# Late attention: how the softmax reciprocals reach the output's rows, by diagonals from GpSimd or by a transpose and one product

## The reference

```python
# kind A: dense, 6 query heads on 2 key heads, normalised and rotated
# kind B: window of 128 tokens to either side, with a sink
m = jnp.maximum(jnp.max(s, axis=-1, keepdims=True), sk)
p = jnp.exp(s - m)
denom = jnp.sum(p, axis=-1, keepdims=True) + jnp.exp(sk - m)
p = p / denom
# kind C: dense, 4 heads, keys from a low-rank projection
p = softmax(s)
# all kinds: o = p v, times silu(gate); then x + concat(oa, ob, oc) @ w_out
```

## Time and profile before

| | us |
|---|---|
| median of three runs | 1826.12 |
| lowest and highest | 1824.75, 1828.1 |
| the profiled execution | 1826.74 |
| its span | 1825.0 |
| PE busy, of the span | 1765.7 |
| DVE busy | 801.9 |
| ACT busy | 723.6 |
| POOL busy | 604.0 |
| mean granted clock of PE | 0.988 |

### The profile page before, as it was taken

How to read it: one execution, slowest core, us unless ns; L and a number is a source line. 1 busy time by engine, 2 the same in 40 slices (tenths; PEclk the granted TensorE clock), 3 DMA queues, 4 the chain that set the end, 5 groups by cost and what they waited for, 6 DMA issues and landing times.

```text
span 1825.0 us, 25256 instructions
## 1 busy us (share of the span) xinstructions
PE 1765.7 (97%) x10862; PEld 1390.1 (76%) x10862; DVE 801.9 (44%) x1342; ACT 723.6 (40%) x1228; POOL 604.0 (33%) x182
## 2 busy tenths in 40 slices
PE   8999999999999999998999999989999999999997
PEld 5778899988888888877888888877684478776456
DVE  8756646623123121114670143145446654526653
ACT  5656665433233332233331222234426533345541
POOL 3534210333333434432454444424332114333112
PEclk9999999999999999998999999989999999999998
DMA  5121200326223323222222232213220012211001
GB/s 205 70 93 24 72 3 25 132 70 191 79 95 104 123 70 110 96 93 69 93 92 93 97 111 93 92 70 140 70 83 10 1 48 97 93 69 47 1 1 47
DMA packets 37504, 144.71 MB, mean 79 GB/s; under 512 B 3155, under 2 KB 15835, under 8 KB 23696
## 3 DMA queue, kind: packets, MB, share of 16 engines
q1 hardware_dynamic: 18944, 121.53, 18.8%
q10 hardware_dynamic: 18448, 21.57, 3.9%
HBM read 140.93 MB, written 5.30 MB: 80 GB/s over the span
## 4 chain that ended last, share of the span: by engine, by line
PE 87%; DVE 5%; ACT 4%; issue 1%; DMA 1%; ACTq 0%; POOL 0%; SPq 0%; POOLq 0%; DVEq 0%
PE bank L407 56%; PE bank L1145 6%; PE bank L613 5%; PE bank L418 4%; PE bank L2196 3%; PE bank L2220 3%; PE bank L2203 2%; DVE WK L978 1%; PE bank L1653 1%; PE bank L1629 1%; PE bank L2149 1%; ACT WK L2330 1%; ACT w_part L365 1%; PE bank L2228 1%; DMA WK<-wgate 1%
## 5 line engine op out<-in xcount | busy, mean ns | idle before, releaser
L407 PE MATMUL bank<-x_part,w_part 128*128 128x512 f32 x3216 | 746.8, 392 | 1.5 <-ACT WK L2309 0.8
L407 PEld LDWEIGHTS bank<-x_part,w_part 128*128 128x128 f32 x3216 | 601.0, 188 | 135.4 <-issue 10.7
L2660 POOL TENSOR_TENSOR w_part<-RAW,w_part 128x2048 fp32r<-128x2048 f32 (+1 forms) x90 | 404.2, 4493 | 678.4 <-ACT w_part L365 678.4
L365 ACT ACTIVATE w_part<-RAW 128x2048 fp32r<-128x2048 f32 (+1 forms) x90 | 165.8, 1842 | 175.5 <-PE bank L407 138.0
L2660 POOL TENSOR_TENSOR w_part<-WK,w_part 128x2048 fp32r<-128x2048 f32 (+1 forms) x30 | 123.7, 4124 | 246.9 <-ACT w_part L365 246.9
L407 PE MATMUL bank<-f_part,w_part 128*128 128x512 f32 x768 | 174.4, 389 | 0.0
L407 PEld LDWEIGHTS bank<-f_part,w_part 128*128 128x128 f32 x768 | 144.1, 188 | 29.9
L1145 PE MATMUL bank<-WK 64*64 64x64 f32 (+1 forms) x1456 | 103.4, 249 | 4.8 <-ACT WK L1311 2.5
L1145 PEld LDWEIGHTS bank<-WK 64*64 64x64 f32 (+1 forms) x1456 | 99.0, 163 | 7.3 <-ACT WK L1311 2.6
L978 DVE SCALAR_TENSOR_TENSOR WK<-bank,COL,WK 128x510 f32<-128x510 f32 (+1 forms) x96 | 71.7, 749 | 48.6 <-ACT WK L920 45.9
L2677 POOL TENSOR_TENSOR WK<-BASE,WK 128x1024 f32<-128x1024 f32 x16 | 30.4, 1898 | 167.5 <-DVE WK L2503 167.5
(11 more groups left out here) (286 smaller groups left out, 2236.1 us busy)
## 6 DMA issues: line engine op xcount, KB each, us to landing
RAW<-wts SPq DMA_DIRECT2D x83, 1024.0 KB, 4.8
WK<-wts SPq DMA_DIRECT2D x23, 1024.0 KB, 4.8
WK<-scratch ACTq DMA_DIRECT2D x16, 256.0 KB, 2.7
WK<-decay_rows ACTq DMA_DIRECT2D x14, 256.0 KB, 6.6
RAW<-wts SPq DMA_DIRECT2D x7, 512.0 KB, 3.5
WK<-wts SPq DMA_DIRECT2D x7, 512.0 KB, 3.4
scratch<-bias_rows ACTq DMA_DIRECT2D x4, 768.0 KB, 8.8
WK<-xT SPq DMA_DIRECT2D x4, 512.0 KB, 7.3
```

What stands on the lines that cost most here:

```text
L365: act.eng.activation(high_part(i), raw_part(i), ACT.Copy).then_inc(*act.did(("hi", i)))
L407: mm = pe.eng.matmul(b[:, :], W[w][:, k, c:c + P], src[x][k], start=start and k == 0 and n == 0, stop=stop and k == kn - 1 and n == 2)
L2660: eng.tensor_tensor(low_part(i), raw_part(i), high_part(i).bitcast(F32), ALU.subtract).then_inc(w_split, 1)
```

## The change

The reciprocals of a pair (128 queries by 8 columns: two heads by four tiles) are no longer spread by diagonals. VectorE splits them into a rounded copy and a remainder, side by side in a 128x16 tile (`INV2`). PE turns that to sixteen rows of 128 (`turn_inverses`, behind the first `av`, round 4m+6). VectorE lays the rows out to 16 rows of 512, each row zero outside its own tile (`inverse_rows`, round 4m+6). One fp32r product with a 16x128 matrix of zeros and ones (`HEAD_OF`) adds the two parts and puts them on the head's 64 rows (`spread`, now in round 4m+8, in front of the last `av`). `gated` moves on to round 4m+9, in front of `out`. The masks are made once per layer in round 1 (`row_masks`). The diagonals and their waits leave POOL's list.

```diff
+            def turn_inverses(m):
+                b = job((L, "rt", m), SPREAD_BANK)
+                pe.wait_ge(*at((L, "ri", m)))
+                E.transpose(b[0:16, 0:P], INV2[m % 2][:, :].bitcast(F32), ident).then_inc(*pe.did(("pe", (L, "rt", m))))
+
             def spread(m):
                 b = job((L, "sp", m), SPREAD_BANK)
-                pe.wait_ge(*at((L, "ridiag", m)))
-                for o in range(2):
-                    mm = E.matmul(b[64 * o:64 * o + 64, :], ones[:, 0:64], SPREAD[:, TT * o:TT * o + TT, :], start=True, stop=True)
-                mm.then_inc(*pe.did(("pe", (L, "sp", m))))
+                pe.wait_ge(*at((L, "rows", m)))
+                E.matmul(b[:, :], HEAD_OF[:, :, :].rearrange("p o c -> p (o c)"), INVR[:, :, :].rearrange("p t c -> p (t c)"), start=True, stop=True)\
+                    .then_inc(*pe.did(("pe", (L, "sp", m))))
...
                 if 0 <= m and u < 3:
                     kind = heads[2 * m][5]
+                    if u == 2:
+                        spread(m)
                     av(m, ((0, 3), (1,), (2,))[u] if kind == "B" else ((0, 1), (2,), (3,))[u])
-                    if u == 1:
-                        spread(m)
+                    if u == 0:
+                        turn_inverses(m)
...
-                    if m >= 2:
-                        dve.wait_ge(*at(("pe", (L, "sp", m - 2))))
...
-                    V.reciprocal(ri, sm).then_inc(*dve.did(*([(L, "ri", m)] if n % 2 else [])))
+                    V.reciprocal(ri, sm).then_inc(*dve.did())
+                both, parts2 = LST[:, 80 + 8 * (m % 2):88 + 8 * (m % 2)], INV2[m % 2]
+                dve.wait_ge(*dve.last())
+                if m >= 2:
+                    dve.wait_ge(*at(("pe", (L, "rt", m - 2))))
+                V.tensor_copy(parts2[:, 0:8], both).then_inc(*dve.did())
+                dve.wait_ge(*dve.last())
+                V.tensor_tensor(parts2[:, 8:16], both, parts2[:, 0:8].bitcast(F32), ALU.subtract).then_inc(*dve.did((L, "ri", m)))
+
+            def row_masks():
+                dve.wait_ge(*at(("pe", (L, "uk", 3))))
+                e16 = ident[0:16, 0:16]
+                V.tensor_reduce(TILE_OF[0:16], e16.rearrange("p (g t) -> p t g", t=TT), AX, ALU.add).then_inc(*dve.did())
+                V.tensor_reduce(QUARTER[0:16], e16.rearrange("p (g t) -> p g t", t=TT), AX, ALU.add).then_inc(*dve.did())
+                dve.wait_ge(*dve.last())
+                first, second = (QUARTER[0:16, 2 * i:2 * i + 2].unsqueeze(2).broadcast_to([16, 2, 64]) for i in range(2))
+                V.tensor_tensor(HEAD_OF[:, :, :], first, second, ALU.add).then_inc(*dve.did())
+
+            def inverse_rows(m):
+                dve.wait_ge(*at(("pe", (L, "rt", m))))
+                V.tensor_tensor(INVR[:, :, :], ps((L, "rt", m))[0:16, 0:P].unsqueeze(1).broadcast_to([16, TT, P]),
+                                TILE_OF[0:16].unsqueeze(2).broadcast_to([16, TT, P]), ALU.mult).then_inc(*dve.did((L, "rows", m), free=(L, "rt", m)))
...
+                    row_masks()
...
-                if i >= 8 and (i - 8) % TT == 0 and (i - 8) // TT < len(heads) // 2:
-                    gated((i - 8) // TT)
+                if i >= 6 and (i - 6) % TT == 0 and (i - 6) // TT < len(heads) // 2:
+                    inverse_rows((i - 6) // TT)
                 if i >= 9 and (i - 9) % TT == 0 and (i - 9) // TT < len(heads) // 2:
+                    gated((i - 9) // TT)
                     out((i - 9) // TT)
...
-            def inverse_diagonal(L, m):
...
-                if subs[i][:2] in last_ahead:
-                    inverse_diagonal(last_ahead[subs[i][:2]], 0)
                 low(i)
-                if subs[i][:2] in last_ahead:
-                    for m in range(1, len(heads) // 2):
-                        inverse_diagonal(last_ahead[subs[i][:2]], m)
```

More of the change, by code:

```diff
@@ L2095, in build @@
         GATE_BANKS = (0, 1, 2, 3), (4, 5, 6, 7)
-        SPREAD = wk(35584, 2 * TT, P)
+        INV2 = [nc.alloc_sbuf_tensor_at(name=f"inverse_sums{i}", shape=[P, 16], dtype=F32R, offset=wk_base + 4 * (37376 + 16 * i)) for i in range(2)]
+        INVR = nc.alloc_sbuf_tensor_at(name="inverse_rows", shape=[16, TT, P], dtype=F32R, offset=wk_base + 4 * 35584)
+        HEAD_OF = nc.alloc_sbuf_tensor_at(name="head_of_row", shape=[16, 2, 64], dtype=F32R, offset=wk_base + 4 * 36096)
+        TILE_OF = wk(36224, 4)
+        QUARTER = wk(36228, 4)
         LGP = wk(12288, 6, S)
```

## The result

The changed kernel takes 1829.39 us in the median of 20 runs (1827.34 to 1833.48); the kernel before, in 20 runs beside them, 1824.18. The ratio is 1.0027, with a 95% interval of 1.0020 to 1.0034: slower by 4.9 us, give or take 1.3. The forecast was no change, 1826.1, with a range up to 1829.3. It stood on the median of three runs of the kernel before, 1826.12, which is 1.9 above the median of 20; counted from one base the forecast missed by the whole 4.9 us.

What follows compares the result with a forecast made beforehand. TensorE held 87% of the chain, but VectorE's lateness set the pace in rounds 1 mod 4. Gains and costs by pair, with masks, summed to -0.02 us a layer, -0.04 in both, on 1826.12: 1826.1 us, range 1822.3 to 1829.3.

Steps and rivals of the forecast that it cites:

- the price of TensorE's two steps: Per pair, product 0.23 us and transpose 0.11 replace the spread's 0.86: 0.52 saved where TensorE sets the pace.
- my sum: All pairs' gains and costs plus masks: -0.02 us a layer, -0.04 in both, giving 1826.1 us.
- three signs of being wrong: Attention's 111.4 us changes by over 1.8; 4m+7 maximum late outside pairs 1, 4, 6; transposes or product over 0.3.
- that wait in pairs 3 and 5: `out` ends 1.0 us later, so `av` begins 0.55 late; less 0.52 saved, cost 0.03 each.
- VectorE's share: Split 0.37 and `gated` 0.7 in 4m+5, some 1.0 us later; `inverse_rows` 0.61 in 4m+6; masks 0.2.
- The late turn in pair 4: ScalarE's copy ends 1.0 us later, so the turn at 1436.70 starts at 1437.68.
- The masks: Three operations once per layer, some 0.6 us, before round 2's maximum, which had 0.44 idle: cost 0.2.
- Pair 7: Gain 0.52; `inverse_rows`' 0.61 fits in an `av` step of 0.86, weight products cover the later `out`.
- Rival 2: VectorE becomes the bound: additions don't overlap in pairs 1, 4 and 6; 9 us slower, 1835.1; chance 0.09.
- Its sign, the lost idle of 1.00 us: It decides where VectorE loses altogether the 1.00 us idle before the maximum at 1436.80.
- Rivals 1, 3 and 4: VectorE all hides, 1817.8, chance 0.11; product not single-pass, 1836.2, 0.02; subtraction meets a POOL split, 1835, 0.02.
- the port: In the tail, without POOL's diagonal, 1.2 us comes back to VectorE's `low`, but TensorE isn't waiting there.

Runs made afterwards that it cites:

- triple: Changed kernel with product and transpose each issued three times: products took 0.90 us, transposes 0.43; attention 118.55 us a layer against 113.30.
- gated_back: Changed kernel with `spread` back in round 4m+7 behind its `av` and `gated` in 4m+8: attention 110.31 us a layer, 1822.47 us, 0.9988 of the kernel before.
- short_rows: Changed kernel with `inverse_rows` of pairs 1 to 7 writing 16x8 elements instead of 16x512: attention 113.29 us a layer against 113.30.
- full128: Changed kernel with the product on 128 rows instead of 16, the added rows zeroed once per layer: attention 111.97 us a layer against 113.30.
- half16_f32: `gated_back` with the product as two float32 halves of 64 columns on 16 rows, directly behind `av`: attention 114.49 us a layer.
- best128: Changed kernel with `gated` in 4m+8, transpose behind turns of 4m+6, 128-row product behind turns of 4m+7: attention 108.54 us, 1819.38 us, 0.9967 of before.
- all128: `best128` with the transpose's weights widened from 16 to 128 columns: attention 108.56 us a layer, 1819.65 us, 0.9973 of the kernel before.
- f32_product: Changed kernel with the product's two tiles read as float32 instead of fp32r: product 1.05 us, attention 118.31 us a layer against 113.30.

## Why the prediction was wrong

**The step that failed** is the price of TensorE's two steps, "I take 0.23, as columns and type are the same as in the 96", and the same for the transpose with 0.11. Both numbers are right for an operation in a stream of its like, and triple confirmed them. Alone between others they cost 0.42 and 0.21. The evidence was in the trace of before, in rows of the chain that I had passed over on the way to round numbers (start, us, what, count):

```profile
1384.80 0.81 PE bank L2203 x6
1385.60 1.01 PE bank L2220 x4
```

Six transposes at 0.11 are 0.65, and the chain gives them 0.81. Two steps of `av` at the price of the spread are 0.86, and it gives them 1.01. The chain counts a group from the end of the one in front, so each of these pays 0.15 for the border in front of it: the turns behind logits of 64 rows, `av` behind the turns. The old spread comes next, behind `av` of the same rows and columns, and so its 0.86 was a price with no border in it. My bounds for the product ran from 0 to 0.86 and held the truth; the value was taken from the wrong row. For the transpose I had called 0.11 the upper bound, and that was false. With 0.42 and 0.21 a pair saves 0.23 and not 0.52.

How much of the miss is this? The layer came out 2.05 above my sum. Eight products at 0.19 are 1.5 of it, and the transposes of the six pairs that pass them on add up to 0.6 at most. With these prices my sum of -0.02 would have been up to +2.1 a layer, and 2.03 was found; the smaller steps below nearly cancel. Two of the forecast's three signs of being wrong came, an attention changed by over 1.8 and a product over 0.3.

**A wait that I left out.** In pairs 1, 4 and 6 the path runs through `gated` and `out` into `av`, which waits 0.38 us for the output bank; I had that wait in pairs 3 and 5 alone. It did little harm there, since the turn behind waited for ScalarE all the same: these pairs lie 0.16, 0.23 and 0.06 above the forecast, where the product's price alone is 0.19. Pairs 3 and 5 lost 0.39 and 0.40. Of the 0.36 beyond the forecast 0.29 is TensorE's price, and the rest is that `av` came 0.62 late instead of 0.55.

**VectorE's share was sized well, but its meaning was missed.** My sum set 4.16 saved on TensorE against 4.1 lost by VectorE's side, masks included. Measured, with 8 x 0.23 = 1.8 saved and 2.03 lost in all, VectorE's side and the rest cost some 3.9. I had written that in 4m+8 VectorE was idle and nothing came back. It should have been read the other way, as free room that the change gave up: gated_back, which moves `gated` and the product with it back, regains 2.99.

**Right.** The late turn in pair 4: forecast 0.98, measured 0.93 (it starts 72.57 us behind the first logits instead of 71.25, and 0.39 of that had come in with the round before). The idle in front of the maximum of round 4m+7 was gone in pairs 1, 4 and 6, as they say. The trace of before shows no engine waiting for one of POOL's diagonals, and none was on the path.

**Right by luck, or wrong without harm.** `inverse_rows` I had falling on the path where VectorE was late, so that the next maximum of pair 4 came 0.54 late. It came 0.64 late, but by another way: short_rows says that `inverse_rows` costs 0.0, and the logits that this maximum needs were themselves 0.64 late, behind the wait of `av` and the transpose. The masks I put at 0.2: the first three turns start 6.88, 9.47 and 11.72 us behind the first logits in both kernels, to 0.01, so they cost nothing. Pair 7 lost 0.61 against its forecast: in the kernel before its `av` and spread ran as one group without borders, 4.44 us from 1472.28; after, the transpose and the product cut it in three, and from 1471.15 it took 4.52 us. In pair 6 the end of the layer gave back more than the 0.25 that I had counted: from its last turns to O0's first product it is 0.85 us where it was 1.34.

**The rivals.** Rival 2 had the sign of the result right. At 9 us it was priced double: the additions overlapped more than it said, and its step of 0.6 for `inverse_rows` doesn't exist. Its sign, the lost idle of 1.00 us, came true but decides nothing, because my own sum lost that idle too. Rivals 1, 3 and 4 did not come about; the longest of the new subtractions took 0.17 us. About the port: no `low` in the changed kernel is a long one any more, and this was worth nothing, as the sum had it.

Left open: what happens in the array in those 0.1 to 0.2 us. The runs show when they are paid, not why. Nor was it tried how much the rounding copy and the subtraction cost by themselves, or what the place of the product is worth apart from that of `gated`.

## What to carry to other kernels

Price a new TensorE step by start to start at its place, not by its rate in a stream: here, between operations with other rows or columns, it cost 0.1 to 0.2 us more, and it can put a second border into a group that ran as one. Not every difference counts, as the list below shows. Where the step could be placed beside operations that it goes with, or padded with zero rows to match them, the border went; here that turned a loss of 0.27% into a gain of 0.33%, together with three steps put elsewhere in their lists. And on an engine that works down a list, an operation moved from an idle round into the one that another engine waits for costs up to its full length, less the slack that is left there: `gated` cost pairs 3 and 5 0.18 each while that slack was whole and 0.6 once it was spent.

## What the runs showed of the hardware

- Between float32 or fp32r products, some changes of the tile cost TensorE time. Between 16 and 128 rows: 0.18 us less for the turns and the product when the product was padded from 16 to 128 rows (full128), and 0.14 more for 16 rows than for 128 behind `av` (half16_f32). From 128 to 64 columns of weights: 0.15, `av` behind the turns (1.01 against 0.86). From 64 rows to 128: 0.15, the turns behind logits (0.81 against 0.65).
- Other changes cost nothing. Eight turns between logits of 96 rows take 0.87 us, the price of a stream, and the transpose of the reciprocals takes 0.12 in front of such logits against 0.21 in front of logits of 64 rows. 16 or 128 columns at the transpose made no difference (best128, all128). Nor did the type: the extra time is 0.18 in fp32r (triple) and 0.19 in float32 (f32_product).
- Rows cost nothing by their number: a product of 512 columns in fp32r takes 0.23 us with 128 rows and 0.24 with 16 (triple).
- On VectorE, 16 partitions were no cheaper than 128: 16x512 took 0.678 us (L2533), 128x512 0.684 (L2540).
- The Trainium skill (SBUF — State Buffer, Who interferes with whom) says that a VectorE instruction with two SBUF inputs and a GpSimd one that reads SBUF exclude each other. The 1.885 us of one `low` beside the last diagonal in the kernel before agrees. No run here had the new subtraction meet a split of POOL.
